# RWKV chunk loop: the next chunk's gram ahead of u, transposes, pairs and w among the levels, level masks at another place

## The chip, the cores and the metric

The kernel runs on 1 core of one Trainium2 chip, in one launch. The metric is the device time of that launch in microseconds (us), the median of three runs. Everything is float32.

## The reference, cut to what matters

Two layers, each with a token mixer and a dense MLP, over T = 1040 tokens of width 1024 (1024 and 16 meta tokens). Half of the mixer is an RWKV-7 recurrence over 8 heads of 64:

```python
def _rwkv7_scan(r, decay, k, v, kk, b):
    """S_t = S_{t-1} diag(decay_t) - (S_{t-1} kk_t) b_t^T + v_t k_t^T ;  y_t = S_t r_t."""
    ...
    def step(S, inp):
        r_t, w_t, k_t, v_t, kk_t, b_t = inp
        sa = jnp.einsum('bhij,bhj->bhi', S, kk_t)
        S = S * w_t[:, :, None, :] - sa[..., None] * b_t[:, :, None, :] + v_t[..., None] * k_t[:, :, None, :]
        y = jnp.einsum('bhij,bhj->bhi', S, r_t)
        return S, y
```

The rest of a layer is the input projection, sparse attention, the output projection and the MLP. The change touches only how this recurrence is computed.

## The kernel before

Each engine has its own instruction stream, written out by hand, and the streams meet in counted semaphores; there is no scheduler. An engine runs its stream in order, so a wait holds everything behind it on that engine.

The recurrence is done in chunks of CH = 64 tokens, NCH = 17 chunks in each of the 2 layers, 34 in all. The 8 heads lie as 4 groups g of two heads (partitions 0 to 63 and 64 to 127). A call of `heads` in `pe_chunk` (L742 records all of its matmuls) is two 64-row matmuls, one for each head of a group; the trace has two matmul records and two weight loads for each matmul, so a call is 4 records. A "half" is two groups: half 0 is g = 0, 1, half 1 is g = 2, 3, each with banks of PSUM of its own, and 8 records make one product over one half.

A chunk in the order of TensorE's stream (`pe_chunk`), with its records:

- gram (32 records, half of them with 128 columns): bh x kr to bank 6, kap x bh to bank 1; then `gram_ready`.
- turned (48): vh, kh and bh transposed to banks 2 and 5 by a product with `ident2`. ScalarE copies them to vk (128x512) and bm (128x256).
- pairs (16, 128 columns): kh x kr to bank 3, once the y of the chunk before is copied out of it (`y_out`).
- levels n = 1 to 5, which double the inverted triangular blocks: X = off x m (half 0, half 1), ScalarE copies X to x, then MX = mt x x (not in level 5) and MT = x x mt of half 0, then of half 1. VectorE subtracts MX from m (L1556) and MT from mt (L1558); in front of each m it masks abt into off (L1555). 48 records in a level, 32 in level 5. In level 1 the products MX wait for `s_out` too, as they overwrite the banks that hold the last chunk's state products.
- w (32): kap x state + akt x vm; ScalarE copies it by halves (L1136). u (16): mt x w, copied the same way.
- state and y (80): km x vm + bm x u to banks 4 and 7, and the three products of y to bank 3; `s_ready` after each half.

VectorE's stream (`dve_chunk`): the new state of half 0 (`new_state`, L1520 and L1522), wait for the gram, the masks abt, m, off, m + identity, mt, mt + identity of each half (L1536 to L1547), the new state of half 1, the levels (with the masks akt, lb, lk, L1562 to L1565, in level 1), and at the end the five operands of the next chunk (`dve_operands`, L1508 to L1510), for which the next gram waits (`bd_ready`). In a level VectorE runs

```python
dve.wait_ge(S["mx_ready"], w.next("mx_ready"))
v.tensor_tensor(off, abt, level[n], ALU.mult)
v.tensor_tensor(m, m, bank2(4, 7, half), ALU.subtract).then_inc(S["m_ready"], 1)
```

`do(...)` issues an instruction and waits until it has finished. ScalarE (`act_chunk`) copies PSUM to SBUF and makes the exponentials of the next chunk (L1116, L1117) in level 1 after `s_out`.

## Time and profile before

| | |
|---|---|
| median of 3 runs | 4112.4 us (4112.28 to 4128.48) |
| the profiled execution | 4112.34 us, its span 4110.5 us |
| TensorE matmul records busy | 3755.0 us, 91% |
| TensorE weight loads busy | 2851.0 us, 69% |
| VectorE, ScalarE, GpSimd busy | 2166.3 us (53%), 870.3 us (21%), 555.6 us (14%) |
| matmul records of the chunk loop (L742) | 15232, from 683.6 us to 3033.0 us |
| mean granted TensorE clock | 0.949 |

The span is the time from the first to the last instruction of the profiled execution; 1.8 us lie around it. The chunk loop stands in it twice, once in each layer, at about 684 to 989 us and 2728 to 3033 us; in between lie the MLP and the next projection and attention. The matmul records overlap each other: the busy time of TensorE counts a stretch as busy in which a new matmul starts every 30 ns, and also the 0.2 us after the last one, so the idle time of the weight loads says more.

### The profile page before, as it was taken

Reading aid. Unit: us, or ns where it says so; the run is one execution under the profiler, and the core shown is the slowest. Engines: PE = TensorE matmul, PEld = TensorE weight load, DVE = VectorE, ACT = ScalarE, POOL = GpSimd, SP = SyncE. Lnnn points to the kernel's source line nnn. Section 1 sums busy time; section 2 is a strip of 40 time slices with the busy share of each in tenths; the row PEclk is TensorE's granted clock in tenths of the full one; section 3 lists DMA queues with packets and bytes.
Section 4 is the critical chain, followed back from the end, with each engine's and each line's share of the span. In section 5 each row is a group of like instructions: output and inputs, shape, how many; then the busy total and the mean of one; then the engine's idle time right before and its main releaser. Section 6 shows DMA issues by size and latency. Waiting matters only on the chain.

```text
span 4110.5 us, 69068 instructions
## 1 busy us (share of the span) xinstructions
PE 3755.0 (91%) x29136; PEld 2851.0 (69%) x29136; DVE 2166.3 (53%) x4280; ACT 870.3 (21%) x1768; POOL 555.6 (14%) x444
## 2 busy tenths in 40 slices
PE   7999887999979999999889998869999799999995
PEld 4566555886548888888655665558865488888884
DVE  2599745666154242434646997466661642434345
ACT  1345462332010000000113446523320100000000
POOL 0041100000011222222100411000000122222220
PEclk9999997999889999999999999879998899999997
DMA  2001100000111111112210110100001111111121
GB/s 111 26 27 41 45 22 1 3 3 26 62 62 42 42 41 42 41 51 84 79 40 21 36 36 23 33 2 3 3 26 67 57 42 41 48 45 41 42 83 52
DMA packets 43384, 163.68 MB, mean 40 GB/s; under 512 B 5056, under 2 KB 5072, under 8 KB 42720
## 3 DMA queue, kind: packets, MB, share of 16 engines
q1 hardware_dynamic: 27648, 100.68, 7.2%
q0 software_dynamic: 15456, 58.85, 3.9%
q8 instruction: 228, 3.74, 0.4%
q14 instruction: 52, 0.43, 0.0%
HBM read 135.07 MB, written 23.49 MB: 39 GB/s over the span
## 4 chain that ended last, share of the span: by engine, by line
PE 73%; DVE 19%; issue 4%; ACT 2%; POOL 1%; DMA 0%; DVEq 0%; ACTq 0%; POOLq 0%
PE ps L712 38%; PE ps L661 9%; PE ps L742 7%; PE ps L629 6%; DVE arena L1425 4%; PE ps L903 2%; PE ps L891 2%; PE ps L916 2%; DVE little L1455 1%; PE ps L945 1%; DVE arena L1556 1%; PE ps L673 1%; PE ps L639 1%; DVE arena L1322 1%; DVE arena L1555 1%
## 5 line engine op out<-in xcount | busy, mean ns | idle before, releaser
L712 PE MATMUL ps<-arena 128*128 128x261 f32 x4096 | 924.7, 383 | 5.7 <-POOL arena L548 2.9
L712 PEld LDWEIGHTS ps<-arena 128*128 128x128 f32 x4096 | 775.1, 189 | 135.1 <-issue 5.4
L661 PE MATMUL ps<-arena,ring 128*128 128x348 f32 x2304 | 704.5, 465 | 37.1 <-DVE arena L1301 18.9
L712 PE MATMUL ps<-arena,ring 128*128 128x261 f32 x3072 | 706.4, 385 | 21.1 <-DVE arena L1778 20.7
L712 PEld LDWEIGHTS ps<-arena,ring 128*128 128x128 f32 x3072 | 585.2, 191 | 122.1 <-issue 21.2
L661 PEld LDWEIGHTS ps<-arena,ring 128*128 128x128 f32 x2304 | 439.0, 193 | 301.4 <-issue 59.6
L742 PE MATMUL ps<-arena 64*64 64x64 f32 (+1 forms) x13600 | 513.0, 226 | 97.8 <-DVE arena L1510 43.2
L742 PEld LDWEIGHTS ps<-arena 64*64 64x64 f32 x13600 | 467.6, 135 | 142.0 <-DVE arena L1556 48.8
L1280 ACT ACTIVATE aux<-ps 128x522 f32<-128x522 f32 x64 | 38.8, 607 | 1535.0 <-PE ps L712 1535.0
L1367 DVE TENSOR_TENSOR arena<-aux,ps 128x522 f32<-128x522 f32 x160 | 111.8, 699 | 423.2 <-PE ps L712 422.7
L548 POOL TENSOR_TENSOR arena<-ring 128x512 f32<-128x512 f32 x128 | 170.1, 1329 | 1106.8 <-DMA ring<-units 1101.4
L1425 DVE TENSOR_SCALAR_CACHE_REDUCE arena<-arena,little 128x384 uint8<-128x384 f32 (+6 forms) x338 | 278.9, 885 | 10.8 <-DVE little L1449 10.7
L1367 DVE TENSOR_TENSOR arena<-arena,ps 128x522 f32<-128x522 f32 x200 | 139.7, 699 | 239.8 <-PE ps L712 237.4
L629 PE MATMUL ps<-arena,ring 128*128 128x348 f32 x768 | 230.1, 463 | 3.7 <-issue 3.7
L629 PEld LDWEIGHTS ps<-arena,ring 128*128 128x128 f32 x768 | 148.4, 194 | 86.3 <-issue 9.8
L1101 ACT ACTIVATE arena<-arena,little 128x1024 bf16<-128x1024 f32 x124 | 142.1, 1146 | 194.4 <-DVEq L1450 194.1
L1644 DVE CUSTOM_DVE_ANT_0 arena<-ps,arena 128x128 f32<-128x128 f32 (+7 forms) x130 | 94.0, 760 | 93.7 <-PE ps L891 84.1
L522 POOL TENSOR_TENSOR arena<-arena 128x1043 f32<-128x1043 f32 x30 | 72.7, 2424 | 474.4 <-ACTq L1080 474.4
L1126 ACT ACTIVATE arena<-ps 128x128 f32<-128x128 f32 x340 | 93.3, 277 | 192.4 <-PE ps L742 192.4
L1310 DVE TENSOR_TENSOR aux<-arena 128x1044 f32<-128x1044 f32 x16 | 19.9, 1246 | 195.6 <-ACT arena L1062 195.6
L639 PE MATMUL ps<-arena,cst 128*128 128x348 f32 x192 | 68.2, 517 | 55.5 <-ACT arena L1055 55.5
L1558 DVE TENSOR_TENSOR arena<-arena,ps 128x128 f32<-128x128 f32 x340 | 95.5, 281 | 30.3 <-PE ps L742 30.3
(228 smaller groups left out, 3674.5 us busy)
## 6 DMA issues: line engine op xcount, KB each, us to landing
ring<-units SPq DMA_DIRECT2D x192, 512.0 KB, 3.7
h_scratch<-arena POOLq DMA_DIRECT2D x24, 522.0 KB, 3.1
arena<-h_scratch POOLq DMA_DIRECT2D x24, 522.0 KB, 8.3
arena<-h_in POOLq DMA_DIRECT2D x16, 522.0 KB, 9.9
out<-arena POOLq DMA_DIRECT2D x8, 522.0 KB, 3.1
arena<-att_scratch POOLq DMA_DIRECT2D x2, 2080.0 KB, 9.3
att_scratch<-arena POOLq DMA_DIRECT2D x16, 256.0 KB, 3.1
aux<-rope POOLq DMA_DIRECT2D x2, 1044.0 KB, 12.5
```

Source lines behind the costliest of these rows:

```text
L548: nc.gpsimd.tensor_tensor(w_sum(p, i), x, y, op).then_inc(S["weights_ready"], 1)
L629: ins = mm(ps[:, b + s, 0:SW], ring[:, (u % RING) * D + k * P:(u % RING) * D + (k + 1) * P], rhs(g * KT + k)[:, slice_(s)], start=(g == 0 ...
L639: ins = mm(ps[:, b + s, 0:SW], const("ones"), sq[k % 2][:, slice_(s)], start=(k == 0), stop=(k == count - 1))
L661: ins = mm(ps[:, b + s, 0:SW], ring[:, r * D + k * P:r * D + (k + 1) * P], tile(U0, k)[:, slice_(s)], start=(k == 0), stop=(k == KT - 1))
L712: ins = mm(acc_at(n)[:, s], lhs[:, k * P:(k + 1) * P], rhs(k)[:, s * HALF:(s + 1) * HALF], start=(k == 0), stop=(k == KT // 2 - 1))
L742: ins = mm(out[r:r + HEAD], lhs[r:r + HEAD], rhs[r:r + HEAD], start=start, stop=stop)
L1101: go(signs[j][0:n], sc(b)[0:n], ACT.Sign, bias=negated[0:n, j:j + 1], scale=1.0, accum_out=sel[0:n, c:c + 1]).then_inc(S["signs_counted"], 1)
L1126: go(cb("x", 256)[:, P * half:P * (half + 1)], ps[:, half, 0:P], ACT.Copy).then_inc(S["x_out"], 1)
L1367: do(v.tensor_tensor(o, x, y, ALU.add))
L1425: v.tensor_scalar(junk[j % 3][0:n, 0:SEL_W[b]], sc(b)[0:n], trial[0:n, c], None, ALU.is_ge, ALU.add, accum_out=count[0:n, c]).then_inc(S[" ...
L1558: v.tensor_tensor(mt, mt, bank2(2, 5, half), ALU.subtract).then_inc(S["mt_ready"], 1)
L1644: v.tensor_tensor_reduce(sm[u % 2][r][:, 0:k], flat[:, c:c + k], mask, -HEAD ** -0.5, 3.0e38, ALU.add, ALU.min, stat[:, at:at + 1])\
```

## The change

- Gram: `pe_gram` of chunk i + 1 is issued in chunk i, behind the copy of w (`w_out`) and in front of u. Chunk 0's stands ahead of the loop.
- Transposes, pairs and w (`pe_beside`) are issued between the products X and MX of levels: pairs in level 2, vh and kh transposed (32 records) in level 3, bh transposed (16) in level 4, w (32) in level 5. They now use banks 6 and 3, behind new semaphores (`gram_used`, `pairs_used`, `km_out`, `b_turned`, `bm_out`). TensorE's records stay the same in number.
- Masks: the mask of off is one instruction of 128x256 for both halves, after `x_ready` of both halves of a level, no longer one of 128x128 in front of each m. akt and lk go to level 2.
- VectorE: at a chunk's start both halves' m and off come first, then both halves' mt (behind `u_mm` of the chunk before, since u reads mt), then the new state of both halves. The operands of the next chunk are spread over levels 3 to 5; bh, in level 5, signals `bd_ready`.
- ScalarE: w is copied by one instruction of 128x256 instead of two; the copy of y comes in level 1 of the next chunk, those of vk and bm in levels 3 and 4.
- State and y: s x rt, vm x lk and km x vm of a half are issued in front of the wait for `u_out`.

The core of the diff (of the lines taken out, those of the first part are not repeated; the kernel above shows them):

```diff
@@ TensorE @@
+            def pe_gram(w, odd):
                 kr = cb4("kr%d" % odd, P)
...
                 pe.wait_ge(S["bd_ready"], w.next("bd_ready"))
                 for g in range(4):
+                    in_quarters(quad(6, g, n=P), bh[:, g], kr[:, g])
+                    ins = in_quarters(quad(1, g), kr[:, g, 0:CH], bh[:, g])
                 ins.then_inc(S["gram_ready"], 1)
...
+            def pe_beside(w, n, odd):
+                kr = cb4("kr%d" % odd, P)
+                if n == 2:
+                    pe.wait_ge(S["y_out"], w.next("y_out"))
+                    for g in range(4):
+                        ins = in_quarters(quad(3, g, n=P), kh[:, g], kr[:, g])
+                    ins.then_inc(S["pairs_ready"], 1)
+                if n == 3:
+                    pe.wait_ge(S["gram_used"], w.next("gram_used"))
+                    for g in range(4):
+                        in_quarters(quad(6, g), vh[:, g], ident2)
+                        ins = in_quarters(quad(6, g, 256), kh[:, g], ident2)
+                    ins.then_inc(S["turned_ready"], 1)
+                if n == 4:
+                    pe.wait_ge(S["pairs_used"], w.next("pairs_used"))
+                    for g in range(4):
+                        ins = in_quarters(quad(3, g), bh[:, g], ident2)
+                    ins.then_inc(S["b_turned"], 1)
+                if n == 5:
+                    pe.wait_ge(S["km_out"], w.next("km_out"))
+                    for g in range(4):
+                        in_quarters(quad(6, g), kr[:, g, 0:CH], s_[:, g], start=True, stop=False)
+                        ins = in_quarters(quad(6, g), akt[:, g], vm[:, g], start=False, stop=True)
+                    ins.then_inc(S["w_ready"], 1)
+            def pe_chunk(w, odd, last=False):
+                rt = cb4("kr%d" % odd, P)[:, :, CH:P]
...
                 for n in range(1, LEVELS):
                     for half in range(2):
                         pe.wait_ge(S["m_ready"], w.next("m_ready"))
                         for g in pairs(half):
+                            ins = in_quarters(half_bank(0, 1, g), off[:, g], m[:, g])
                         ins.then_inc(S["x_ready"], 1)
+                    pe_beside(w, n, odd)
                     if n == 1:
                         pe.wait_ge(S["s_out"], w.next("s_out", 2))
...
                         pe.wait_ge(S["mt_ready"], w.next("mt_ready"))
                         if n < LEVELS - 1:
                             for g in pairs(half):
+                                ins = in_quarters(half_bank(4, 7, g), mt[:, g], x[:, g])
                             ins.then_inc(S["mx_ready"], 1)
                         for g in pairs(half):
+                            ins = in_quarters(half_bank(2, 5, g), x[:, g], mt[:, g])
                         ins.then_inc(S["mx_ready"], 1)
+                pe.wait_ge(S["w_out"], w.next("w_out"))
+                if not last:
+                    pe_gram(w, 1 - odd)
+                for half in range(2):
+                    pe.wait_ge(S["mt_ready"], w.next("mt_ready"))
+                    for g in pairs(half):
+                        ins = in_quarters(half_bank(2, 5, g), mt[:, g], akt[:, g])
+                    ins.then_inc(S["u_mm"], 1)
+                pe.wait_ge(S["bm_out"], w.next("bm_out"))
                 for half in range(2):
                     for g in pairs(half):
+                        y = quad(3, g)
+                        in_quarters(y, s_[:, g], rt[:, g], start=True, stop=False)
+                        in_quarters(y, vm[:, g], lk[:, g], start=False, stop=False)
+                        in_quarters(half_bank(4, 7, g), km[:, g], vm[:, g], start=True, stop=False)
+                        if g % 2 == 0:
+                            pe.wait_ge(S["u_out"], w.next("u_out"))
+                        in_quarters(half_bank(4, 7, g), bm[:, g], u_[:, g], start=False, stop=True)
+                        ins = in_quarters(y, u_[:, g], lb[:, g], start=False, stop=True)
                     ins.then_inc(S["s_ready"], 1)
             def pe_chunks(w):
+                pe_gram(w, 0)
                 for c in range(NCH):
-                    pe_chunk(w, c % 2)
+                    pe_chunk(w, c % 2, last=c == NCH - 1)
             pe.wait_ge(S["consts_in"], 32)
@@ ScalarE @@
+            def y_copy(w, i):
+                act.wait_ge(S["s_ready"], w.next("s_ready", 2))
+                go(four(X_Y0, ZW)[:, :, bass.ds(i * CH, CH)], bank4(3, CH), ACT.Copy).then_inc(S["y_out"], 1)
+            def act_chunk(w, i, odd, first=False, last=False):
                 for n in range(1, LEVELS):
                     for half in range(2):
                         act.wait_ge(S["x_ready"], w.next("x_ready"))
                         go(cb("x", 256)[:, P * half:P * (half + 1)], ps[:, half, 0:P],
                            ACT.Copy).then_inc(S["x_out"], 1)
                     if n == 1:
+                        if not first:
+                            y_copy(w, i - 1)
                         act.wait_ge(S["s_out"], w.next("s_out", 2))
                         if not last:
                             act_factors(w, i + 1, 1 - odd)
+                    if n == 3:
+                        act.wait_ge(S["turned_ready"], w.next("turned_ready"))
+                        go(cb("vk", 512), ps[:, 6, :], ACT.Copy).then_inc(S["km_out"], 1)
+                    if n == 4:
+                        act.wait_ge(S["b_turned"], w.next("b_turned"))
+                        go(cb("bm", 256), ps[:, 3, 0:256], ACT.Copy, scale=-1.0).then_inc(S["bm_out"], 1)
+                act.wait_ge(S["w_ready"], w.next("w_ready"))
+                go(cb("akt", 256), ps[:, 6, 0:256], ACT.Copy).then_inc(S["w_out"], 1)
+                for half, b in ((0, 2), (1, 5)):
+                    act.wait_ge(S["u_mm"], w.next("u_mm"))
+                    go(cb("u", 256)[:, P * half:P * (half + 1)], ps[:, b, 0:P], ACT.Copy).then_inc(S["u_out"], 1)
             act.wait_ge(S["consts_in"], 32)
             for l in range(DEPTH):
@@ VectorE @@
-                    new_state(w, 1 - odd, 0)
                 dve.wait_ge(S["gram_ready"], w.next("gram_ready"))
+                v.tensor_tensor(cb4("abt"), bank4(6, P)[:, :, 0:CH], over4(const("strict")), ALU.mult)\
+                    .then_inc(S["dve_done"], 1)
+                abt_done = w.next("dve_done")
                 for half in range(2):
-                    m, mt, off, abt = (half2(n, half) for n in ("m", "mt", "off", "abt"))
-                    if half == 0:
-                        v.tensor_tensor(cb4("abt"), bank4(6, P)[:, :, 0:CH], over4(const("strict")), ALU.mult)\
-                            .then_inc(S["dve_done"], 1)
-                        abt_done = w.next("dve_done")
+                    m = half2("m", half)
                     v.tensor_tensor(m, bank4(1, CH)[:, 2 * half:2 * half + 2], over2(const("inv0")), ALU.mult)\
                         .then_inc(S["dve_done"], 1)
                     m_done = w.next("dve_done")
-                    dve.wait_ge(S["dve_done"], abt_done)
-                    v.tensor_tensor(off, abt, level[0], ALU.mult)
+                    if half == 0:
+                        dve.wait_ge(S["dve_done"], abt_done)
+                        v.tensor_tensor(cb4("off"), cb4("abt"), level(0), ALU.mult)
                     dve.wait_ge(S["dve_done"], m_done)
                     v.tensor_tensor(m, m, over2(ident2), ALU.add).then_inc(S["m_ready"], 1)
-                    do(v.tensor_tensor(mt, abt, over2(const("inv0t")), ALU.mult))
+                for half in range(2):
+                    mt = half2("mt", half)
+                    if not first:
+                        dve.wait_ge(S["u_mm"], w.next("u_mm"))
+                    do(v.tensor_tensor(mt, half2("abt", half), over2(const("inv0t")), ALU.mult))
                     v.tensor_tensor(mt, mt, over2(ident2), ALU.add).then_inc(S["mt_ready"], 1)
                 if not first:
+                    new_state(w, 1 - odd, 0)
                     new_state(w, 1 - odd, 1)
                 for n in range(1, LEVELS):
+                    dve.wait_ge(S["x_ready"], w.next("x_ready", 2))
+                    if n < LEVELS - 1:
+                        v.tensor_tensor(cb4("off"), cb4("abt"), level(n), ALU.mult)
+                    if n == 2:
+                        dve.wait_ge(S["pairs_ready"], w.next("pairs_ready"))
+                        v.tensor_tensor(cb4("akt"), bank4(3, P)[:, :, 0:CH], over4(const("strict")), ALU.mult)
+                    if n == 3 and not last:
+                        dve.wait_ge(S["exp_ready"], w.next("exp_ready"))
+                        dve_operand(i + 1, 1 - odd, "kap")
+                    if n == 4 and not last:
+                        dve.wait_ge(S["turned_ready"], w.next("turned_ready"))
+                        dve_operand(i + 1, 1 - odd, "kh")
+                    if n == 5 and not last:
+                        dve.wait_ge(S["b_turned"], w.next("b_turned"))
+                        dve_operand(i + 1, 1 - odd, "bh").then_inc(S["bd_ready"], 1)
                     for half in range(2):
-                        m, mt, off, abt = (half2(k, half) for k in ("m", "mt", "off", "abt"))
+                        m, mt = (half2(k, half) for k in ("m", "mt"))
                         if n < LEVELS - 1:
                             dve.wait_ge(S["mx_ready"], w.next("mx_ready"))
-                            v.tensor_tensor(off, abt, level[n], ALU.mult)
                             v.tensor_tensor(m, m, bank2(4, 7, half), ALU.subtract).then_inc(S["m_ready"], 1)
                         dve.wait_ge(S["mx_ready"], w.next("mx_ready"))
                         v.tensor_tensor(mt, mt, bank2(2, 5, half), ALU.subtract).then_inc(S["mt_ready"], 1)
-                        if n == 1:
-                            if half == 0:
-                                dve.wait_ge(S["pairs_ready"], w.next("pairs_ready"))
-                                v.tensor_tensor(cb4("akt"), bank4(3, P)[:, :, 0:CH], over4(const("strict")), ALU.mult)
-                            else:
-                                v.tensor_tensor(cb4("lb"), bank4(6, P)[:, :, CH:P], over4(const("nincl")), ALU.mult)
-                                v.tensor_tensor(cb4("lk"), bank4(3, P)[:, :, CH:P], over4(const("incl")), ALU.mult)
-                if not last:
-                    dve_operands(w, i + 1, 1 - odd)
+                    if n == 1:
+                        v.tensor_tensor(cb4("lb"), bank4(6, P)[:, :, CH:P], over4(const("nincl")), ALU.mult)\
+                            .then_inc(S["gram_used"], 1)
+                    if n == 2:
+                        v.tensor_tensor(cb4("lk"), bank4(3, P)[:, :, CH:P], over4(const("incl")), ALU.mult)\
+                            .then_inc(S["pairs_used"], 1)
+                    if n == 3 and not last:
+                        dve_operand(i + 1, 1 - odd, "rt")
+                    if n == 4 and not last:
+                        dve_operand(i + 1, 1 - odd, "vh")
             dve.wait_ge(S["consts_in"], 32)
             for l in range(DEPTH):
```

## Rows read from the trace of the kernel before

**Rows 1.** The page: span, granted clock in 40 slices, weight loads of the loop.

```profile
span 4110.5 us, 69068 instructions
...
PEclk9999997999889999999999999879998899999997
...
L742 PEld LDWEIGHTS ps<-arena 64*64 64x64 f32 x13600 | 467.6, 135 | 142.0 <-DVE arena L1556 48.8
```
**Rows 2.** Windows of one chunk: start:end, length, then busy (count) by engine.

```profile
core 0: us, PE busy (x) PEld busy (x) DVE busy (x) ACT busy (x) POOL busy (x), PEclk, DMA share, GB/s
807.72:810.10 2.38, 2.38 (x84) 2.38 (x82) 0.74 (x3) 0.28 (x1) 0.00 (x0) 1.00 0.03 7
810.10:811.44 1.34, 1.34 (x38) 1.34 (x36) 0.00 (x0) 0.38 (x1) 0.00 (x0) 1.00 0.00 0
811.44:812.84 1.40, 1.40 (x54) 1.40 (x52) 1.18 (x5) 0.00 (x0) 0.00 (x0) 1.00 0.00 0
812.84:813.72 0.88, 0.88 (x22) 0.88 (x20) 0.84 (x5) 0.66 (x2) 0.00 (x0) 1.00 0.09 19
813.72:814.18 0.46, 0.46 (x20) 0.46 (x16) 0.42 (x3) 0.23 (x2) 0.00 (x0) 1.00 0.00 0
811.39:829.20 17.81, 16.20 (x452) 14.97 (x450) 11.89 (x49) 5.81 (x19) 0.00 (x0) 1.00 0.01 3
```
**Rows 3.** Timeline of levels: start, length, engine, line, count, idle before.

```profile
817.62 0.29 DVE L1555 TENSOR_TENSOR arena<-arena,cst 128x128 f32<-128x128 f32 x1
817.83 0.28 DVE L1556 TENSOR_TENSOR arena<-arena,ps 128x128 f32<-128x128 f32 x1
818.02 0.28 DVE L1558 TENSOR_TENSOR arena<-arena,ps 128x128 f32<-128x128 f32 x1
818.22 0.28 DVE L1555 TENSOR_TENSOR arena<-arena,cst 128x128 f32<-128x128 f32 x1
818.42 0.28 DVE L1556 TENSOR_TENSOR arena<-arena,ps 128x128 f32<-128x128 f32 x1
...
818.76 1.60 PEld L742 LDWEIGHTS ps<-arena 64*64 64x64 f32 x48 [0.27 <-DVE arena L1556]
...
819.50 0.29 DVE L1555 TENSOR_TENSOR arena<-arena,cst 128x128 f32<-128x128 f32 x1 [0.60 <-PE ps L742]
...
820.64 1.60 PEld L742 LDWEIGHTS ps<-arena 64*64 64x64 f32 x48 [0.28 <-DVE arena L1556]
```
**Rows 4.** Timeline of a chunk's start: y copy, masks, state, first MX.

```profile
810.43 0.38 ACT L1139 ACTIVATE arena<-ps 128x256 f32 x1 [2.29 <-PE ps L742]
...
811.66 0.42 DVE L1536 TENSOR_TENSOR arena<-ps,cst 128x256 f32<-128x256 f32 x1 [1.89 <-PE ps L742]
812.00 0.28 DVE L1539 TENSOR_TENSOR arena<-ps,cst 128x128 f32<-128x128 f32 x1
...
812.60 0.28 DVE L1546 TENSOR_TENSOR arena<-arena,cst 128x128 f32<-128x128 f32 x1
...
812.92 0.29 DVE L1547 TENSOR_TENSOR arena<-arena,cst 128x128 f32<-128x128 f32 x1
...
814.26 0.28 DVE L1520 TENSOR_TENSOR arena<-arena,ps 128x128 f32<-128x128 f32 x1
814.57 0.29 DVE L1522 TENSOR_TENSOR arena<-arena 128x128 f32<-128x128 f32 x1
814.91 1.35 PEld L742 LDWEIGHTS ps<-arena 64*64 64x64 f32 x40 [0.70 <-DVE arena L1522]
...
814.99 0.42 ACT L1116 ACTIVATE arena<-arena 128x256 f32 x1 [0.31 <-DVE arena L1522]
```
**Rows 5.** Timeline of TensorE alone at the first chunk of layer 1.

```profile
683.62 2.83 PE L742 MATMUL ps<-arena 64*64 64x128 f32 x32 [16.58 <-DVE arena L1510]
686.21 2.27 PE L742 MATMUL ps<-cst,arena 64*64 64x64 f32 x48
...
689.99 0.41 PE L742 MATMUL ps<-arena 64*64 64x64 f32 x7 [0.18 <-issue]
```

More of the change, by code:

```diff
@@ L292, in trunk @@
             "lora_in", "lora_ready", "lora_out", "kk_in", "kk_sq", "kk_sums", "kk_max", "kk_inv", "kk_ready", "kk_out", "heads_in",
-            "rwkv_in", "scan_ready", "exp_ready", "bd_ready", "gram_ready", "turned_ready", "pairs_ready", "km_out", "m_ready", "mt_ready", "x_ready", "x_out",
+            "rwkv_in", "scan_ready", "exp_ready", "bd_ready", "gram_ready", "gram_used", "turned_ready", "pairs_ready", "pairs_used", "km_out",
+            "b_turned", "bm_out", "m_ready", "mt_ready", "x_ready", "x_out",
             "mx_ready", "w_ready", "w_out", "u_mm", "u_out", "s_ready", "s_out", "y_out", "rwkv_done",
@@ L761, in pe_chunk @@
+            def pe_chunk(w, odd, last=False):
+                rt = cb4("kr%d" % odd, P)[:, :, CH:P]
+                pairs = lambda half: (2 * half, 2 * half + 1)
                 for n in range(1, LEVELS):
@@ L1132, in act_chunk @@
                             act_factors(w, i + 1, 1 - odd)
-                for ready, dst, b, done in (("w_ready", "x", (0, 1), "w_out"), ("u_mm", "u", (2, 5), "u_out")):
-                    for half in range(2):
-                        act.wait_ge(S[ready], w.next(ready))
-                        go(cb(dst, 256)[:, P * half:P * (half + 1)], ps[:, b[half], 0:P],
-                           ACT.Copy).then_inc(S[done], 1)
-                act.wait_ge(S["s_ready"], w.next("s_ready", 2))
-                go(four(X_Y0, ZW)[:, :, bass.ds(i * CH, CH)], bank4(3, CH), ACT.Copy).then_inc(S["y_out"], 1)
+                    if n == 3:
[9 more added lines that the diff above has]
+                    go(cb("u", 256)[:, P * half:P * (half + 1)], ps[:, b, 0:P], ACT.Copy).then_inc(S["u_out"], 1)
             act.wait_ge(S["consts_in"], 32)
@@ L1256, in _ @@
                 act_factors(w, 0, 0)
-                with w.loop(NCH // 2, s_out=4, turned_ready=2, x_ready=4 * (LEVELS - 1), w_ready=4, u_mm=4,
+                act_chunk(w, 0, 0, first=True)
+                with w.loop((NCH - 3) // 2, s_out=4, turned_ready=2, b_turned=2, x_ready=4 * (LEVELS - 1), w_ready=2, u_mm=4,
                             s_ready=4) as i:
-                    act_chunk(w, i * 2, 0)
                     act_chunk(w, i * 2 + 1, 1)
+                    act_chunk(w, i * 2 + 2, 0)
+                act_chunk(w, NCH - 2, 1)
                 act_chunk(w, NCH - 1, 0, last=True)
+                y_copy(w, NCH - 1)
                 for g in range(4):
@@ L1722, in _ @@
                 dve.sem_inc(S["rwkv_in"], 1)
-                dve_operands(w, 0, 0)
+                dve.wait_ge(S["exp_ready"], w.next("exp_ready"))
+                for name in ("kap", "rt", "kh", "vh"):
+                    dve_operand(0, 0, name)
+                dve_operand(0, 0, "bh").then_inc(S["bd_ready"], 1)
                 assert NCH % 2
                 dve_chunk(w, 0, 0, first=True)
-                with w.loop((NCH - 3) // 2, exp_ready=2, gram_ready=2, pairs_ready=2, mx_ready=2 * (4 * LEVELS - 6),
-                            s_ready=4, s_out=4, dve_done=2 * 7) as i:
+                with w.loop((NCH - 3) // 2, exp_ready=2, gram_ready=2, pairs_ready=2, x_ready=4 * (LEVELS - 1),
+                            mx_ready=2 * (4 * LEVELS - 6), turned_ready=2, b_turned=2, u_mm=4, s_ready=4, s_out=4,
+                            dve_done=2 * 7) as i:
                     dve_chunk(w, i * 2 + 1, 1)
@@ L1731, in _ @@
                 dve_chunk(w, NCH - 1, 0, last=True)
+                w.skip("u_mm", 2)
+                w.skip("turned_ready", 1)
+                w.skip("b_turned", 1)
                 new_state(w, 0, 0)
```

82 lines of the change are left out of this document (19 added, 63 removed).

## Prediction

> **What bounds the kernel now.** I read the page first, for the size of the loop and the clock; then windows, for the time of each product block; then the timelines of one level and of a chunk's start, for what ends each wait. The loop is 34 chunks of 17.81 us [rows 2], some 605 us of the 4110.5 us span [rows 1]; nothing else changes. The page gives the idle time in front of the loop's weight loads: 142.0 us [rows 1], over 34 chunks 4.2 us each. That is what a new order can win at most, since the same 448 records have to run.
>
> What do the records cost by themselves? The windows are cut where TensorE runs without a gap [rows 2] (their counts include neighbours that end inside). State and y, 80 records, take 2.38 us; gram, 32, 1.34; the transposes, 48, 1.40; pairs, 16 of 128 columns, 0.88; both X of a level, 16, 0.46. So a 64-column record costs 0.029 us and a block of 8 takes 0.23. A chunk is then 2.38 + 1.34 + 1.40 + 0.88, four levels of 48 records at 1.39, level 5 and w at 0.93 each, u at 0.46: 13.88 us. The other 3.93 of the 17.81 us are waits.
>
> The level's timeline shows the chain that sets them [rows 3]. X of half 1 starts at 818.76; MX of half 0 follows; VectorE starts on it at 819.50. Then come off, m, mt, off, m, one every 0.20 us (817.62 to 818.42 in the level before), and 0.06 us after the last one's end, 818.42 + 0.28, TensorE starts the next X of half 1. A level lasts 1.88 us (818.76 to 820.64), of which 1.39 are records. At the chunk's start the chain is VectorE's too [rows 4]: abt starts 0.22 us after the gram's last record (811.44 to 811.66), and the new state of half 1, which comes behind all masks, ends at 814.86; TensorE has run out of records at 814.18 [rows 2] and starts MX at 814.91: 0.73 us.
>
> **Unit costs for the new order**, from [rows 2 to 4]: TensorE's end of a block to a VectorE or ScalarE start 0.22; either engine's end to a TensorE start 0.055. VectorE start to start: 0.20 behind a 128-wide instruction, 0.34 behind a 256-wide one (811.66 to 812.00), 0.32 if the second waits for the first's result (812.60 to 812.92, 814.26 to 814.57). A 128-wide one ends after 0.28, a 256-wide ScalarE copy after 0.38.
>
> **Levels 1 to 4.** The mask of off now runs while TensorE computes MX: X of half 1 ends at 0.23 (from its start), off runs from 0.45 to 0.79, and MX of half 0 is ready for VectorE at 0.68 or, with a block B put in front, 0.68 + B. What comes last is m of half 1: X 0.23, B, MX and MT of half 0 0.46, MX of half 1 0.23, 0.22 to VectorE, m 0.28, back 0.055: 1.48 + B. The records themselves take 1.39 + B, so TensorE still waits 0.09 us per level, against 0.49 before.
> - Level 2, B = pairs 0.88. Here VectorE is later: pairs end at 1.11, akt starts at 1.33, m, mt, m at 1.67, 1.87, 2.07, next X at 2.41.
> - Level 3, B = 32 records, 0.93: 2.41. kap is hidden by it, rt comes after the last mt, while TensorE runs the next X.
> - Level 4, B = 16 records, 0.46: 1.94. kh is hidden in the same way.
> - Level 1, no B, but MX waits for the state. From MX: 1.48 - 0.23 = 1.25.
>
> **Level 5 and gram.** X 0.23, w 0.93, then ScalarE: 0.22 + 0.38 + 0.055, so the gram starts at 1.82; both MT (0.46) lie inside that. The gram ends at 3.16. bh, for which it waits, starts at 0.45: hidden. mt of half 1 is ready by 2.2, before u wants it.
>
> **Gram end to MX of level 1.** TensorE has u 0.46, state and y 2.38, X 0.46 here, 3.30 us. VectorE has a chain from `gram_ready`: abt 0.34, m 0.20, off 0.34, m+I 0.20, m of half 1 0.32 (its m+I waits for it), m+I 0.20, twice mt 0.32 and mt+I 0.20 (the last 0.21): 2.65; then the state, add 0.32, product 0.42 (its wait, and register work as in front of ScalarE's L1116, which starts 0.13 after the state's end where TensorE needs 0.05 [rows 4]), add 0.32, product 0.29: 4.00. With 0.22 and 0.055 that is 4.28 us. So the state of half 0, which was done ahead of the masks, now stands in line behind them, and TensorE waits 4.28 - 3.30 = 0.98 us where it waited 0.73. This stall I expect to stay and to be the largest left. The mt masks wait for `u_mm`, ready 0.7 us after the gram: not last. The copy of y and the exponentials fall into the same stretch on ScalarE and end over 0.2 us before the next x copy.
>
> **Sum.** 4.28 + 1.25 + 2.41 + 2.41 + 1.94 + 3.16 = 15.45 us a chunk, against 17.81: 2.36 less. From one MX of level 1 to the next there are 16 such steps in each layer: 37.8 us. The first chunk: before, 683.62 to 689.99 [rows 5], 6.37 us, from the gram to MX. The gram takes 2.59 there (to 686.21), at a lower clock; after it the new chunk needs only VectorE's masks to mt+I of half 0, 0.22 + 2.20 + 0.055: 5.07, a gain of 1.3. The last chunk has no gram to fill its waits: 12.8 against 13.0 us, 0.2. A layer gains 39.3, the two layers 78.6. The profiled execution took 4112.34 us and the median is 4112.4, so the one stands for the other: **4034 us**.
>
> A rule on VectorE speaks for a longer chain. In the Trainium skill, "VectorE: DVE Perf Modes", section "The DRAIN you can't avoid", the next instruction does not start until the pipeline is empty, and a semaphore on each costs nothing extra. Here L1539 starts 0.34 us after a 0.42 us instruction, and a dependent one starts 0.12 us later than an independent one [rows 4, 3], so both halves of it differ from this trace. By it, each step would last its full duration, the chain 4.56 us instead of 4.28, and the time be 4043 us. I go by the rows.
>
> **Unknown costs, both ends.** VectorE gets some ten more waits per chunk against values in registers (`x_ready` five times, `u_mm` twice, `exp_ready`, `turned_ready`, `b_turned`). Lower end nothing, as in the levels, where such work is done while the instruction before runs; upper end 0.08 us each, the difference of 0.13 and 0.05 above, all on the path: 0.8 x 34 = 27 us. I take nothing, as most stand in levels where TensorE's B covers them. ScalarE's two peeled chunks and the loop's jump come at places with slack; upper end a delay of one copy, 0.38 us [rows 4], every second chunk, 6 us; lower end nothing; taken nothing.
>
> **The rivals.**
> - *VectorE's new waits are serial* (above): 15.45 + 0.8; 4055 to 4065 us. For it: VectorE's stream sets the largest stall. Against it: its busy time is 11.89 of 17.81 us [rows 2]. Chance 0.13.
> - *TensorE sets the pace at the state, too*: were the masks done by the time `s_ready` comes, the chain behind state and y would be 0.22 + 0.32 + 0.29 + 0.055 = 0.89, the stretch 0.46 + 2.38 + 0.89 = 3.73, 0.55 less a chunk: 4016 us. It needs VectorE's chain 0.55 shorter than its rows say. Chance 0.08.
> - *The change does not do what it says*: if the matmul records' busy 16.20 us of a chunk [rows 2], and not my 13.88, were TensorE's real work, it would stay 16.20, and with the stalls that I still count, 15.45 - 13.88 = 1.57, a chunk is 17.8: 4110 us. For it: the window counts it as busy; against it the windows without a gap, and that 16.20 counts each burst's last 0.2 us. Chance 0.05.
> - *Slower*: the clock. The records depend on the granted clock, which is 1.00 in the chunk [rows 2] and 9 in the page's slices of the loop [rows 1], though TensorE waits 3.93 us per chunk in pieces up to 0.73. The new order has one piece of 0.98. If that made the clock fall to 1.2 GHz, each chunk's 13.88 us would double. The first gram, 2.59 against 1.34 us, shows the price [rows 5, 2]. It decides from (78.6 + 20.6) / 13.9 = 7 of the 34 chunks on; at 10 of them the time is 4034 + 139 = 4173 us. Against it: less idle in all than before. Chance 0.02.
> - The forecast, 4020 to 4050 us, has 0.72.
>
> **Range and chances.** A measurement of this kernel tells about 0.5%, 20.6 us, from no change. The range holds the forecast's own, the faster rival and the serial waits: 4012 to 4068. Faster by over 0.5% (below 4092) 0.93; within it 0.05; slower 0.02.
>
> **What would show it.** A period of 15.4 to 15.5 us between the same instructions of two chunks; levels 2, 3, 4 of 2.4, 2.4, 1.9 us; TensorE's largest wait in front of MX of level 1, released by the state's product, 0.9 to 1.0 us; idle time in front of the weight loads near 1.6 to 1.9 us a chunk, 55 to 65 us in all, instead of 142; the gram without a wait for `bd_ready`. I would be wrong if blocks B stretch the levels by more than their own records, if the gram waits for an operand, or if VectorE's chain from gram to state is not in 0.34, 0.20 and 0.32 steps.

## The result, and the profile after

The changed kernel takes 4067.7 us in the median of 4 runs (4055.1 to 4071.7). The four runs of before that go with them have a median of 4115.9 us (4112.3 to 4128.5). The ratio is 0.987, 95% interval 0.985 to 0.990: faster by 1.3%, 48 us, where 79 us and 4034 us were forecast. 4067.7 is inside the range of 4012 to 4068 by 0.3 us, and outside the 4020 to 4050 us that the forecast itself was given.

The profiled execution took 4055.1 us. Three parts of its page (L739 is what L742 was in the kernel before, the line that records all matmuls of the loop):

```profile
span 4053.3 us, 68954 instructions
...
PEclk9999995999889999999999999879989899999998
...
L739 PEld LDWEIGHTS ps<-arena 64*64 64x64 f32 x13600 | 452.1, 136 | 91.6 <-issue 45.5
```

The idle time in front of the loop's weight loads fell from 142.0 us [rows 1] to 91.6. The releaser named, "issue 45.5", is new at the head of the list, and the view of this one line shows why it needs care. It counts the waits of weight loads and of matmuls together, so a wait can stand in it twice. After the change:

```profile
its engine sat idle before it (us, times) until:
  DVE arena L1546: 51.8, 64
  issue: 45.5, 3
  DVE arena L1535: 43.3, 2
```

The timelines say where the 45.5 us lie. First the kernel before, then the changed one, each at the first gram of the two layers:

```profile
683.59 2.67 PEld L742 LDWEIGHTS ps<-arena 64*64 64x64 f32 x32 [17.58 <-issue]
2727.62 2.67 PEld L742 LDWEIGHTS ps<-arena 64*64 64x64 f32 x32 [27.66 <-issue]
...
692.19 2.67 PEld L739 LDWEIGHTS ps<-arena 64*64 64x64 f32 x32 [17.59 <-issue]
2703.06 2.67 PEld L739 LDWEIGHTS ps<-arena 64*64 64x64 f32 x32 [27.66 <-issue]
```

45.2 us in each kernel are TensorE's wait ahead of the first gram of each layer, for the work in front of the loop. So the 142.0 us of the kernel before were some 97 us within the loops, 2.9 us a chunk, not 4.2. Within the loops the idle time fell by half, to 46 us, 1.4 a chunk.

The windows give the chunk, cut at abt, MX of level 1, and X of half 1 in levels 2 to 5 (columns as in [rows 2]):

```profile
core 0: us, PE busy (x) PEld busy (x) DVE busy (x) ACT busy (x) POOL busy (x), PEclk, DMA share, GB/s
805.32:809.28 3.96, 3.22 (x111) 3.08 (x106) 3.70 (x14) 1.33 (x5) 0.00 (x0) 1.00 0.02 4
809.28:810.59 1.31, 1.30 (x40) 1.25 (x41) 1.23 (x5) 0.72 (x2) 0.00 (x0) 1.00 0.00 0
810.59:813.03 2.44, 2.44 (x68) 2.35 (x65) 1.99 (x8) 0.55 (x2) 0.00 (x0) 1.00 0.04 7
813.03:815.50 2.47, 2.47 (x82) 2.41 (x80) 2.05 (x8) 1.15 (x3) 0.00 (x0) 1.00 0.00 0
815.50:817.51 2.01, 2.01 (x69) 1.95 (x65) 2.01 (x8) 0.94 (x3) 0.00 (x0) 1.00 0.03 8
817.51:820.97 3.46, 3.44 (x100) 3.31 (x98) 1.32 (x5) 0.94 (x3) 0.00 (x0) 1.00 0.02 5
805.32:820.97 15.65, 14.89 (x455) 14.35 (x452) 12.31 (x44) 5.63 (x18) 0.00 (x0) 1.00 0.02 4
```

The period of a chunk, from one abt to the next, is 15.65 us (forecast 15.45). Before it lasted 17.81 [rows 2], which alternates with 17.88 over the chunks of the loop, mean 17.85. The timeline of the same chunk:

```profile
805.32 0.42 DVE L1555 TENSOR_TENSOR arena<-ps,cst 128x256 f32<-128x256 f32 x1 [1.28 <-PE ps L739]
...
807.97 0.28 DVE L1544 TENSOR_TENSOR arena<-arena,ps 128x128 f32<-128x128 f32 x1
808.29 0.29 DVE L1546 TENSOR_TENSOR arena<-arena 128x128 f32<-128x128 f32 x1
...
808.62 0.29 DVE L1544 TENSOR_TENSOR arena<-arena,ps 128x128 f32<-128x128 f32 x1
...
808.94 0.29 DVE L1546 TENSOR_TENSOR arena<-arena 128x128 f32<-128x128 f32 x1
809.28 4.06 PEld L739 LDWEIGHTS ps<-arena 64*64 64x64 f32 x112 [0.88 <-DVE arena L1546]
...
811.96 0.42 DVE L1584 TENSOR_TENSOR arena<-ps,cst 128x256 f32<-128x256 f32 x1 [0.45 <-PE ps L739]
...
812.69 0.28 DVE L1598 TENSOR_TENSOR arena<-arena,ps 128x128 f32<-128x128 f32 x1
...
813.31 1.10 PE L739 MATMUL ps<-cst,arena 64*64 64x64 f32 x32
...
814.25 1.71 PE L739 MATMUL ps<-arena 64*64 64x64 f32 x48
...
814.69 0.29 DVE L1598 TENSOR_TENSOR arena<-arena,ps 128x128 f32<-128x128 f32 x1 [0.41 <-PE ps L739]
...
818.94 0.38 ACT L1162 ACTIVATE arena<-ps 128x256 f32<-128x256 f32 x1 [0.66 <-PE ps L739]
...
819.37 4.69 PEld L739 LDWEIGHTS ps<-arena 64*64 64x64 f32 x144 [0.15 <-ACT arena L1162]
```

VectorE works without a pause from abt (805.32) through both states to 809.23, and TensorE, out of records, waits 0.88 us for the last decay product: the one large stall left, at the place and of the releaser that were forecast (0.98). From there on TensorE has hardly a gap: the view names pauses from 0.15 us on, and behind 809.28 it names one in the weight loads, 0.15 us for the copy of w.

Where did the rest of the gain go? The same stretches of the whole span, before and after: the time ahead of the first loop, the loop of layer 1, what lies between the loops, the loop of layer 2, and the rest. Before:

```profile
0.00:683.60 683.60, 595.60 (x2768) 369.82 (x2769) 437.66 (x853) 285.19 (x501) 91.28 (x67) 0.93 0.12 41
683.60:989.90 306.30, 278.10 (x7617) 256.85 (x7617) 200.56 (x829) 98.32 (x321) 0.00 (x0) 0.99 0.01 3
989.90:2727.60 1737.70, 1603.42 (x6964) 1170.15 (x6964) 889.01 (x1318) 337.90 (x564) 275.58 (x215) 0.94 0.13 45
2727.60:3034.10 306.50, 278.37 (x7617) 257.16 (x7617) 200.87 (x829) 98.32 (x321) 0.00 (x0) 0.99 0.01 3
3034.10:4110.50 1076.40, 999.48 (x4172) 796.98 (x4172) 438.18 (x453) 50.58 (x61) 188.77 (x162) 0.94 0.15 52
```

After:

```profile
0.00:692.20 692.20, 604.80 (x2768) 374.03 (x2769) 437.62 (x853) 285.37 (x501) 91.70 (x67) 0.92 0.12 40
692.20:964.90 272.70, 257.74 (x7617) 248.38 (x7617) 208.30 (x744) 94.72 (x304) 0.00 (x0) 0.98 0.02 4
964.90:2703.10 1738.20, 1603.67 (x6966) 1170.21 (x6966) 888.30 (x1318) 338.02 (x564) 275.50 (x215) 0.94 0.13 45
2703.10:2973.20 270.10, 255.31 (x7617) 245.67 (x7617) 207.57 (x743) 94.73 (x304) 0.00 (x0) 0.99 0.02 4
2973.20:4053.30 1080.10, 1002.63 (x4172) 797.53 (x4172) 435.46 (x453) 50.59 (x61) 189.08 (x162) 0.94 0.14 52
```

The two loops together fell from 612.8 to 542.8 us: 70.0 us. The code outside, the same in both, took 3510.5 us instead of 3497.7. 8.6 of these 12.8 us come ahead of the first loop, where both kernels have the same work (2768 matmul records and 853 VectorE instructions in each) and the mean granted clock is 0.92 instead of 0.93.

### The profile page after: what moved, and what is told of

Same layout as the page of the kernel before. It is cut to its first block, busy times and chain, and to the rows that moved or that the text cites. A ratio compares the mean times of both kernels' runs of the same rounds, so it can differ in the third digit from the quotient of the medians.

```text
span 4053.3 us, 68954 instructions
## 1 busy us (share of the span) xinstructions
PE 3724.1 (92%) x29136; PEld 2835.8 (70%) x29136; DVE 2177.3 (54%) x4110; ACT 863.4 (21%) x1734; POOL 556.3 (14%) x444
## 4 chain that ended last, share of the span: by engine, by line
PE 77%; DVE 16%; issue 3%; ACT 2%; POOL 1%; DMA 0%; DVEq 0%; ACTq 0%; POOLq 0%
PE ps L713 38%; PE ps L739 10%; PE ps L662 9%; PE ps L630 6%; DVE arena L1454 4%; PE ps L922 2%; PE ps L910 2%; PE ps L964 1%; DVE little L1484 1%; PE ps L935 1%; PE ps L674 1%; PE ps L640 1%; DVE arena L1351 1%; DVE arena L1358 1%; ACT arena L1238 1%
## 5 line engine op out<-in xcount | busy, mean ns | idle before, releaser
L662 PE MATMUL ps<-arena,ring 128*128 128x348 f32 x2304 | 705.1, 465 | 36.4 <-DVE arena L1330 18.9
L739 PE MATMUL ps<-arena 64*64 64x64 f32 (+1 forms) x13600 | 476.7, 225 | 70.9 <-DVE arena L1535 43.3
L739 PEld LDWEIGHTS ps<-arena 64*64 64x64 f32 x13600 | 452.1, 136 | 91.6 <-issue 45.5
```

The lines of the kernel that those rows point to most:

```text
L662: ins = mm(ps[:, b + s, 0:SW], ring[:, r * D + k * P:r * D + (k + 1) * P], tile(U0, k)[:, slice_(s)], start=(k == 0), stop=(k == KT - 1))
L739: ins = mm(out[r:r + HEAD], lhs[r:r + HEAD], rhs[r:r + HEAD], start=start, stop=stop)
```

## The experiments

Two questions were open: whether the forecast's chain is what sets a chunk, and what the time outside the loops goes by.

**The changed kernel once more.** No edit.

> The changed kernel once more, unchanged. What is open: its loops are 70.0 us shorter than before (306.3 + 306.4 against 272.6 + 270.1 us), but the profiled execution is only 57 us shorter and the median 48, and the code outside the loops took 3510.5 us against 3497.8. Theory A (a draw): the time outside the loops goes by how long TensorE's clock is granted at half there, which differs from one execution to the next of the same kernel; then the five times here spread over some 15 us again, the lower clock with the longer time, and the outside can also come out below 3510. Theory B (systematic): the new loop leaves the code around it in a worse clock each time; then the outside is 3510 us or more in this run and in every kernel with the new loop. Both: period of a chunk 15.65 us.

Median 4065.3 us (5 runs, 4063.1 to 4069.4) against 4128.5 us for before on that chip (9 runs, 4112.9 to 4131.9); ratio 0.985 (0.983 to 0.987). Period 15.65 us, loops 272.6 and 270.1 again, outside 3521.3 us. The loops repeat to 0.1 us, the outside moved by 11. That the outside stays above 3510 would fit either theory; it is before's own runs that now spread.

**The kernel before, twice more.** No edit.

> The kernel before once more, unchanged, for the place of its outside time. The profiled execution of before took 3497.8 us outside the two loops, those of the kernels with a shorter loop 3510 to 3521, also in the 684 us ahead of the first loop, where no instruction differs. Theory A (a draw of the clock in each execution): this one, if it takes 4120 us or more, has the longer outside too, with TensorE's clock at half for longer there and loops of the same 306.3 us. Theory B (only the new kernels have it): outside within 3 us of 3497.8 whatever its total.

> A second repetition of the kernel before, to the same question: loops 306.3 us each; if its total differs from before_again's, the difference lies outside the loops and is half of the difference in half-clock time (Theory A).

The two profiled executions took 4113 us (span 4111.3) and 4130 us (span 4128.1); only the second is one of the longer executions that the question is about. Both have loops of 306.0 to 306.6 us. Outside them they took 3498.5 and 3516.2 us. The slower of them, ahead of its first loop and between its loops:

```profile
0.00:691.80 691.80, 604.20 (x2768) 373.61 (x2769) 437.78 (x853) 285.55 (x501) 91.93 (x67) 0.92 0.12 40
...
997.80:2746.70 1748.90, 1614.30 (x6965) 1175.23 (x6965) 891.97 (x1318) 338.23 (x564) 275.25 (x215) 0.94 0.13 45
```

Its first stretch, 691.8 us at a clock of 0.92, is the changed kernel's 692.2 and not the 683.6 of the same kernel's first profile. So what Theory A says does happen: the time outside differs from one execution of a kernel to the next, and the clock with it. The mean granted clock of the span was 0.949 in the execution of 4110.5 us and 0.946 in that of 4128.1. At half speed for a share 2 x (1 - clock) of the span, that is 419 and 446 us; half of the difference, 13 us, is most of the 17.6 us, the clock being given to three digits only. The 49 executions of before with a clock on record fall in line: 0.949 to 0.951 in the 13 under 4115 us, 0.945 or 0.946 in the 19 over 4127. Over all 52 timed executions of before, on several chips, the times run from 4111.2 to 4131.9 us, 14 of them under 4115 and 21 over 4125, mean 4122.2. The 4112.4 us that the prediction started from were a draw at the short end.

Theory A is not the whole account, though. As an estimate, with the loops taken from the profiles, the rest of each time is what lies outside them. On one chip before's 15 executions have 3497 to 3511 us there, and the ten of masks alone (below), whose loops are the old ones but for the masks, have 3516 to 3524. On another, before's nine have 3498 to 3517 and the changed kernel's five 3518 to 3525. Theory B as it was put falls too: with the new loop, state by half and x ahead of y (both below) come down to 3499 and 3495 us in single executions.

**Masks alone.** The old order, with one part of the change:

```diff
                 for n in range(1, LEVELS):
+                    dve.wait_ge(S["x_ready"], w.next("x_ready", 2))
+                    if n < LEVELS - 1:
+                        v.tensor_tensor(cb4("off"), cb4("abt"), over4(const("levels")[:, n * CH:(n + 1) * CH]), ALU.mult)
                     for half in range(2):
...
                         if n < LEVELS - 1:
                             dve.wait_ge(S["mx_ready"], w.next("mx_ready"))
-                            v.tensor_tensor(off, abt, level[n], ALU.mult)
```

> The kernel before with one part of the change alone: the mask of off in levels 1 to 4 is one 128x256 instruction behind X instead of one 128x128 in front of each m. Theory 1 (in the old order it is VectorE's five instructions that time a level): then X, the copy of x by ScalarE, MX and one subtraction of half 1 remain, 0.28 + 0.56 + 0.28 + 0.56 = 1.67 us against 1.88 in levels 2 to 4, and level 1 loses 0.36: period 16.9 against 17.85, both loops 34 us shorter, not quite half of the whole change. Rival (masks count for little without the work spread among the levels, as TensorE or ScalarE times them anyway): period above 17.4.

Period 17.13 us (17.16 and 17.10 in turn), loops 293.7 and 293.3 us, 25.8 us less than before; forecast 34. The off masks of levels 3 and 4 show a level:

```profile
823.04 0.42 DVE L1553 TENSOR_TENSOR arena<-arena,cst 128x256 f32<-128x256 f32 x1 [0.36 <-PE ps L742]
...
824.78 0.42 DVE L1553 TENSOR_TENSOR arena<-arena,cst 128x256 f32<-128x256 f32 x1 [0.32 <-PE ps L742]
```

1.74 us a level against 1.88: VectorE now waits for TensorE, 0.32 us, where TensorE waited for VectorE. So VectorE's five instructions timed the old level. The chain over ScalarE's copy follows 0.14 behind: the copy of x of half 0 runs from 824.40 to 824.68, and MX of half 0 starts at 824.73. It stands between the two expectations, nearer to Theory 1, and brings somewhat over a third of the loops' gain. The total hardly shows it: 4110.7 us against 4119.6, ratio 0.998 (0.997 to 0.999), since this kernel's outside was 3517.5 us.

**Operands at the end.** The changed kernel with the operands put together again:

```diff
-                    if n == 5 and not last:
-                        dve.wait_ge(S["b_turned"], w.next("b_turned"))
-                        dve_operand(i + 1, 1 - odd, "bh").then_inc(S["bd_ready"], 1)
...
+                if not last:
+                    for sem in ("exp_ready", "turned_ready", "b_turned"):
+                        dve.wait_ge(S[sem], w.next(sem))
+                    for name in ("kap", "rt", "kh", "vh"):
+                        dve_operand(i + 1, 1 - odd, name)
+                    dve_operand(i + 1, 1 - odd, "bh").then_inc(S["bd_ready"], 1)
```

> The changed kernel with one part undone: the five operands of the next chunk are made together behind the last mt of level 5, as before, not spread over levels 3 to 5. Theory 1 (the gram ahead of u pays only if its operands are ready): bh comes 1.6 us behind the last mt, the gram starts 3.9 us after X of level 5 instead of 1.9, and u, state and y wait behind it: period 17.65, both loops within 8 us of before; all of the gain is gone. Rival (the operands' place is of little weight, TensorE has other work meanwhile): period below 16.3.

4140.6 us (4 runs), ratio 1.005 (1.004 to 1.007): slightly slower than before. The shortest periods are 17.7 to 17.8 us (forecast 17.65); the loops take 310.0 and 311.0 us, 8.3 us more than before. TensorE's wait ahead of the gram:

```profile
798.51 4.71 PEld L739 LDWEIGHTS ps<-arena 64*64 64x64 f32 x144 [2.26 <-issue]
798.54 4.82 PE L739 MATMUL ps<-arena 64*64 64x128 f32 x144 [2.15 <-DVE arena L1535]
```

The releaser is the last operand (L1535), 2.15 us after the last MT. Theory 1 is right on the place and the size: the gram ahead of u is worth nothing without the spread of the operands. And something was not expected: every few chunks one or two last 18.1 to 18.9 us instead of 17.8. There the granted clock falls inside the loop, which it does not do in before or in the changed kernel once the first 20 us of a loop are over:

```profile
697.00:745.00 48.00, 40.16 (x1202) 38.84 (x1200) 32.59 (x116) 14.80 (x47) 0.00 (x0) 0.99 0.01 4
745.00:749.00 4.00, 4.00 (x85) 4.00 (x83) 2.85 (x11) 0.55 (x2) 0.00 (x0) 0.57 0.02 4
```

**mt and state interleaved.** In the mt and state steps no VectorE instruction waits for the one in front of it any more:

```diff
-                    do(v.tensor_tensor(mt, half2("abt", half), over2(const("inv0t")), ALU.mult))
-                    v.tensor_tensor(mt, mt, over2(ident2), ALU.add).then_inc(S["mt_ready"], 1)
+                    v.tensor_tensor(mt, half2("abt", half), over2(const("inv0t")), ALU.mult).then_inc(S["dve_done"], 1)
+                    mt_done.append(w.next("dve_done"))
+                for half in range(2):
+                    dve.wait_ge(S["dve_done"], mt_done[half])
+                    mt = half2("mt", half)
+                    v.tensor_tensor(mt, mt, over2(ident2), ALU.add).then_inc(S["mt_ready"], 1)
...
+                        v.tensor_tensor(s_, s_, bank2(4, 7, half), ALU.add).then_inc(S["dve_done"], 1)
+                        added.append(w.next("dve_done"))
```

> VectorE's stretch from gram to state reordered: both mt products, then both mt + identity; both state additions, then both decay products, so that no instruction waits for the one in front of it. Theory 1 (VectorE's chain from gram to state sets the stall in front of MX of level 1): the chain from abt's start to that MX falls from 3.96 us to 3.58, the period from 15.65 to 15.27, the loops lose 12 us together. Rival (TensorE's own records and the signal behind state and y set it, the chain only looks late): period stays 15.65.

Period 15.245 us (forecast 15.27), loops 264.4 and 264.4 us, total 4041.5 us, ratio 0.980 (0.978 to 0.983). The stall in front of MX:

```profile
813.16 4.05 PEld L739 LDWEIGHTS ps<-arena 64*64 64x64 f32 x112 [0.47 <-DVE arena L1591]
```

0.47 us instead of 0.88: the 0.41 us taken from VectorE's chain are 0.41 us of the chunk. The chain sets it; the rival falls.

**Pairs in level 1.** The pairs go into that stall:

```diff
-                if n == 2:
+                if n == 1:
                     pe.wait_ge(S["y_out"], w.next("y_out"))
...
             def act_chunk(w, i, odd, first=False, last=False):
+                if not first:
+                    y_copy(w, i - 1)
                 for n in range(1, LEVELS):
```

> The pairs move from level 2 into the stall of level 1 (between X and MX); for that ScalarE copies y ahead of the x of level 1, and akt is masked behind the last mt of level 2. Theory 1 (the stall there is an idle TensorE that work can fill): gram end to MX grows from 4.18 to 4.43 us as the pairs wait for the copy of y, level 2 falls from 2.44 to 1.63: period 15.09, both loops 18 us shorter. Rival (what is put in front of MX only moves: the stall is given back elsewhere, as x copies or masks come late): period 15.5 or more.

Period 15.23 us, loops 264.4 and 264.9 us, ratio 0.981 (0.979 to 0.983), 4046.1 us. Filling the stall brings 0.42 us a chunk where 0.56 were forecast, and the rival's 15.5 is not reached. The wait that remains:

```profile
803.50 4.25 PEld L739 LDWEIGHTS ps<-arena 64*64 64x64 f32 x112 [0.27 <-ACT arena L1141]
```

It is now for the copy of y.

**State by half.** MX of a half waits for its own state only, on top of the interleaved mt:

```diff
-                    if n == 1:
-                        pe.wait_ge(S["s_out"], w.next("s_out", 2))
                     for half in range(2):
+                        if n == 1:
+                            pe.wait_ge(S["s_out"], w.next("s_out"))
```

> MX of level 1 waits for the new state of its own half only, the state of half 0 is finished before that of half 1 is begun, and the mt steps are interleaved. Theory 1 (VectorE's chain): MX of half 0 can start 3.1 us after abt's start, where TensorE just runs out of records, MX of half 1 at 3.6, the next X of half 1 at 4.5 instead of 5.3: period 14.9 us, both loops 24 us shorter, about 4030 us if the outside stays at 3510. Rival (TensorE's restart costs and ScalarE's copies of x set it): less than half of that, period above 15.3.

Period 15.10 us, loops 261.9 and 263.5 us, ratio 0.977 (0.975 to 0.979), 4035.5 us. It falls between the theories: 0.55 us won of the 0.75 forecast. The first block after the stall:

```profile
801.38 0.51 ACT L1147 ACTIVATE arena<-ps 128x128 f32<-128x128 f32 x2 [2.30 <-PE ps L739]
...
801.72 4.08 PEld L739 LDWEIGHTS ps<-arena 64*64 64x64 f32 x112 [0.30 <-issue]
```

ScalarE can copy x of half 0 only at 801.38, when X is done; 801.38 + 0.28 + 0.06 = 801.72. My forecast had TensorE start MX as soon as it ran out of records and left that copy out.

**X ahead of y.** So X of the next level 1 goes ahead of most of the y products, with the state in two buffers, since y still reads the old one:

```diff
+                y_in(0, (0,))
+                for g in range(4):
+                    in_quarters(half_bank(4, 7, g), km[:, g], vm[:, g], start=True, stop=False)
+                    if g % 2 == 0:
+                        pe.wait_ge(S["u_out"], w.next("u_out"))
+                    ins = in_quarters(half_bank(4, 7, g), bm[:, g], u_[:, g], start=False, stop=True)
...
+                if not last:
+                    pe_x(w)
+                for g in range(1, 4):
+                    ins = y_in(g, (0, 1))
+                ins.then_inc(S["y_ready"], 1)
```

> On top of state_by_half (15.10 us a chunk): the state products of all groups come ahead of the y products of groups 1 to 3, X of the next chunk's level 1 stands between them, and the state has two buffers, so that ScalarE's copy of x and VectorE's state lie under the y products. In state_by_half MX of level 1 waited 0.30 us for the copy of x. Theory 1 (that copy, and a restart of TensorE, which costs 0.05 us, are what is left there): period 14.8, both loops about 10 us shorter than in state_by_half. Rival (VectorE is the next to be late, its state now ends with nothing to spare): 15.0 or more.

Period 14.90 us, loops 259.9 and 258.8 us (6.7 less than in state_by_half, 10 forecast), 4031.6 us, ratio 0.978 (0.976 to 0.979). The view, which names pauses from 0.15 us on, shows no wait of TensorE between its gram and level 3:

```profile
799.93 7.93 PEld L739 LDWEIGHTS ps<-arena 64*64 64x64 f32 x234
```

Its loops are the shortest of all, 94.1 us below before. Between this kernel and state_by_half the totals cannot tell, both being 2.2 to 2.3% faster than before; the loops can.

## Why the prediction was near, step by step

The mechanism is right and the time is not: 4034 us were forecast, 4067.7 measured. Of the 33.9 us between them the loops make 8.6 (70.0 won instead of 78.6), and the code outside them the other 25 (3497.8 us in the profile that the forecast starts from, 3523 in the median of the changed kernel). That 4067.7 lies in the range is luck: the range reached up to 4068 for the serial waits (4055 to 4065 us), which no run shows, and not for what happened outside the loops.

- **The loop's gain is there.** 70.0 us of the forecast 78.6, by the mechanisms named: shorter levels, work in the waits, one stall left in front of MX of level 1, released by the state. Of the signs named, the gram without a wait for its operands came as said and the levels within 0.1 us; the period, 15.65, is beyond 15.4 to 15.5; the stall, 0.88, is just under 0.9.
- **Masks, levels 2 to 4.** Forecast 2.41, 2.41, 1.94; measured 2.44, 2.47, 2.01.
- **Level 1 from MX**: 1.25 forecast, 1.31 measured. **Level 5 and gram**, 3.16 forecast: 817.51 to 820.75, 3.24 (820.97 less the 0.22 to VectorE).
- **Gram end to MX**: 4.28 forecast, 0.22 + 3.96 = 4.18 measured. The register work of 0.1 us between the two states, which I had added, did not come: 808.29 to 808.62 is 0.33.
- **The mis-sized term in the period** is the first block behind a wait. I took 0.23 us for every 8 records. After a wait it is 0.28: X of level 3 may start at 813.03 (812.69 + 0.28 + 0.06), and the next product starts at 813.31, while the following 32 records take 0.94, 0.235 per 8. TensorE restarts six times in a chunk (X in levels 2 to 5, MX in level 1, the gram); as an estimate, 6 x 0.05 = 0.30, less the 0.10 above: 0.20, as much as 15.65 differs from 15.45.
- **Period and edges together.** 32 x 2.20 = 70.4 us, so the first and the last chunks bring nothing in sum where I had 3.0. The 2.20 is the 2.36 forecast less the 0.20 above, and 0.04 more because a chunk of before lasts 17.85 in the mean and not 17.81. In layer 1 the loop brought 33.6 us, in layer 2 36.3. In layer 1 the clock stayed at 1.2 GHz (0.50 over 692.2 to 702.2 us) for all of the loop's first 10 us, in before for less (0.80 over its first 10 us), and in layer 2 it was 0.84. That the sparser first chunk kept it low is a guess: no run separates it.
- **The step that failed** is "the one stands for the other": the profiled execution and the median of 4112 us for the kernel before. They were draws at the short end of 4111 to 4132, and with "nothing else changes" the sum put the time outside the loops at the 3497.8 us of that one execution without a reason. Against before's mean of 4122.2 us over 52 executions, the changed kernel's mean of 4065.6 over nine is 56.5 less. The loops' 70.0 are not all seen in it, since the nine have on average 3521 us outside, and the 52 of before 3508. Masks alone has 3521 too (ten executions, loops as in its profile), operands at the end 3517, pairs in level 1 3517, the interleaved kernel 3513, state by half 3508, x ahead of y 3507. So it does not go by how short the loop is. That executions of one kernel differ is shown; why some kernels have more outside on average, on one chip without overlap, stays open, as no run held the rest equal.
- **New waits of VectorE**: taken at nothing, and nothing was seen of them. The rival of 0.8 us a chunk falls: in the gram-to-state stretch the steps are 0.20 to 0.21 or 0.31 to 0.34.
- **The Trainium skill's rule** ("VectorE: DVE Perf Modes", "The DRAIN you can't avoid") was taken for more than it says. It adds that a next op that is not held starts earlier, and the interleaved 128-wide instructions, 0.20 us apart at 0.28 us each, agree with that. That a semaphore costs nothing extra does not fit here: taking away the waits of the mt and state steps took 0.41 us off the chunk.
- **TensorE at the state** (4016 us): not so in the changed kernel, where the stall was 0.88 us; interleaving shows that it was VectorE's chain. **TensorE really busy 16.20 us**: refuted, the chunk takes 15.65 and even 14.90 with the same records.
- **The clock as a slower case**: not in the changed kernel. But the clock can fall inside the loop: with the operands at the end, where TensorE waits 2.26 us once in each chunk, it did, and with longest waits of 0.73 (before) and 0.88 us (changed) it did not. Whether the one long wait or the idle time in all does it is not separated: the weight loads' idle time is 3.2 us a chunk there (153.8 us on its page, less the 45 ahead of the loops), 2.9 in before, 1.4 in the changed kernel.
- **142.0 us idle over 34 chunks** was a misreading: 45 of it lie ahead of the loops. So the 55 to 65 us expected after the change came out as 91.6 on the page and 46 within the loops. Nor is 2.9 us a chunk the most that a new order can win: x ahead of y won 2.95 and its weight loads still idle 0.55 (63.9 us on its page, less the 45). The 3.93 us from the windows, which count the records alone, were the better bound.

## What to carry to other kernels

Price a new order by walking it block by block with start-to-start times from the trace, and give each block that follows a wait its restart cost. Spreading work into waits pays only if its operands are spread too. Then take the difference from the loops' own windows, and not from totals: before a saving of one or two percent is forecast in total time, look at how far executions of the same kernel lie apart, and in which stretch, and say what the unchanged stretches are expected to do.

## What the runs showed of the hardware that was not expected

- The same kernel takes 4111 to 4132 us, and two profiled executions of it differ by 17.7 us outside the loops and by under 1 us within them, with a mean granted TensorE clock of 0.949 and 0.946. On one chip two kernels lay apart outside their loops without overlap (3497 to 3511 us in before, 3516 to 3524 in masks alone, worked out with the loops of the profiles).
- TensorE needs 0.05 us more for the first block behind a wait (0.28 against 0.23 us for 8 records, at 813.03 us of the changed kernel).
- With a wait of 2.26 us once in a chunk of 17.8 us the granted clock fell inside a loop again and again (0.57 over 745 to 749 us); with longest waits of 0.73 and 0.88 us it did not. One kernel shows it, and the idle time in all is longer there too.
